# First embedding gate reordered by token tile, a new beginning without the spread row, and conv taps on TensorE in groups of ten

## What is computed

```python
h = rms_norm(x, pre_norm_g[0])                    # the beginning
z = h @ ret_w_in                                  # the heads: q, k, v, gate
a = einsum('bhid,bhjd->bhij', qb, kb) * dmask     # masked products of a head
...
x = x + rms_norm(y, post_norm_g[i])
x = x + (p[i] @ ple_w_proj[i]) * sigmoid(x @ ple_w_gate[i])   # the embedding gate
h = rms_norm(x, pre_norm_g[1]);  z = h @ mla_w_in             # what follows the first gate
...
ya = a_val * sigmoid(a_gate)
ya = causal_dwconv(ya, w_dw_a, b_dw_a)            # 31 taps, 512 channels = 4 tiles of 128
ya = silu(layer_norm(ya)) @ w_pw_a
ga, gb = sigmoid(gate_a), sigmoid(gate_b)         # gate strips: columns of the same w_in
```

## Time and profile before

| | |
|---|---|
| median of 3 runs | 875.16 us (875.09 to 876.24) |
| the profiled execution | 875.0 us, its span 873.2 us |
| granted clock of TensorE, mean | 0.996 |
| busy: PE, PEld, DVE, ACT, POOL | 858.1, 781.1, 662.8, 492.7, 50.3 us |
| first matmul of the span | at 1.33 us |
| read from HBM | 167.95 MB, 194 GB/s over the span |

### The profile page before, as it was taken

The page is one execution under the profiler, slowest core; times in us unless marked ns, Lnnn a source line. Parts: engine busy times, 40 slices in busy tenths (PEclk is TensorE's granted clock), DMA queues, the critical chain, the costliest instruction groups (busy, mean ns, idle before and its releaser), DMA issues.

```text
span 873.2 us, 15801 instructions
## 1 busy us (share of the span) xinstructions
PE 858.1 (98%) x5676; PEld 781.1 (89%) x5676; DVE 662.8 (76%) x928; ACT 492.7 (56%) x732; POOL 50.3 (6%) x61
## 2 busy tenths in 40 slices
PE   9999999999999999999999999999999999999995
PEld 7898999988868999999988889999998999999884
DVE  6869777686865786877866876899898788888566
ACT  5454545544646656656565446455753698888440
POOL 0018000000012000000000000070000000000000
PEclk9999999999999999999999999999999999999998
DMA  7857575669554656473738662634444465556541
GB/s 245 307 190 236 191 247 176 232 234 340 177 178 156 227 168 233 132 254 112 259 121 319 230 220 85 208 120 146 145 157 181 134 228 176 184 184 228 193 166 48
DMA packets 48433, 169.60 MB, mean 194 GB/s; under 512 B 5507, under 2 KB 6147, under 8 KB 48390
## 3 DMA queue, kind: packets, MB, share of 16 engines
q1 hardware_dynamic: 40612, 142.70, 48.2%
q10 hardware_dynamic: 7778, 26.32, 8.4%
HBM read 167.95 MB, written 1.05 MB: 194 GB/s over the span
## 4 chain that ended last, share of the span: by engine, by line
PE 87%; DVE 8%; ACT 2%; issue 2%; ACTq 0%; POOL 0%; DVEq 0%; POOLq 0%
PE bank L445 14%; PE bank L446 14%; PE bank L447 14%; PE bank L491 8%; PE bank L493 8%; PE bank L492 8%; PE bank L458 3%; PE bank L534 2%; PE bank L858 2%; DVE wlo L1441 1%; PE bank L766 1%; PE bank L654 1%; PE bank L655 1%; PE bank L656 1%; PE bank L769 1%
## 5 line engine op out<-in xcount | busy, mean ns | idle before, releaser
L934 ACT ACTIVATE whi<-raw 128x1024 fp32r<-128x1024 f32 (+1 forms) x251 | 259.6, 1040 | 223.7 <-PE bank L447 106.7
L1441 DVE TENSOR_TENSOR wlo<-raw,whi 128x1024 fp32r<-128x1024 f32 (+1 forms) x251 | 301.8, 1212 | 91.8 <-ACT whi L934 89.4
L445 PE MATMUL bank<-H,whi 128*128 128x256 f32 x904 | 261.6, 289 | 0.0
L447 PE MATMUL bank<-H,wlo 128*128 128x256 f32 x904 | 255.7, 283 | 0.0
L446 PE MATMUL bank<-H,whi 128*128 128x256 f32 x904 | 255.6, 283 | 0.0
L445 PEld LDWEIGHTS bank<-H,whi 128*128 128x128 f32 x904 | 173.2, 192 | 1.0 <-issue 0.4
L446 PEld LDWEIGHTS bank<-H,whi 128*128 128x128 f32 x904 | 173.3, 192 | 0.5
L447 PEld LDWEIGHTS bank<-H,wlo 128*128 128x128 f32 x904 | 173.1, 192 | 0.0
L491 PE MATMUL bank<-whi,Y 128*128 128x512 f32 x216 | 84.2, 390 | 0.0
L493 PE MATMUL bank<-whi,Y 128*128 128x512 f32 x216 | 84.1, 389 | 0.0
L492 PE MATMUL bank<-wlo,Y 128*128 128x512 f32 x216 | 84.1, 389 | 0.0
(11 more groups left out here) (259 smaller groups left out, 1310.6 us busy)
## 6 DMA issues: line engine op xcount, KB each, us to landing
ada_raw<-ada_in ACTq DMA_DIRECT2D x48, 512.0 KB, 5.2
raw<-w_head SPq DMA_DIRECT2D x47, 512.0 KB, 4.5
raw<-w_up SPq DMA_DIRECT2D x42, 512.0 KB, 3.4
...
```

The lines of the kernel that those rows point to most:

```text
L445: mm(o, whi[:, s, c], a[:, 0, :], start=start, stop=False)
L447: last = mm(o, wlo[:, s, c], a[:, 0, :], start=False, stop=stop)
L934: activation(whi[:, s, 0:n], block_in(b, n), ACT.Copy).then_inc(hi_done, 1)
L1441: tt(wlo[:, s, 0:n], block_in(b, n), f32(whi[:, s, 0:n]), ALU.subtract).then_inc(lo_done, 1)
```

## The change

1. The beginning. The spread row is gone (`row_spread`, L619). The gain of the first norm comes as 8 columns (`pre`, 128 x 8), and is applied after the transposes, when they are copied out of PSUM, as a scale per partition: four activations and four tensor_scalar per tile in place of one copy each. DVE scales X by the reciprocal alone. TensorE's `hold` runs 20 matmuls in a row. ACT and DVE split block 5 before the sine tables are waited for.
2. The heads. In each pass of the loop three blocks of the next head are split at its end in place of two, the two ada steps move back by one or two splits, and the mask of the head's product stands ahead of the split of block 11.
3. The first embedding gate. Tile 0 runs over both column halves (eight blocks), then tile 1. The split parts of blocks +4 to +7 (KEPT) lie in `Y`, which is free there, in place of the ring. The transposes of tile 0 for the next product stand between the second and third of tile 1's last four blocks. The order on ACT and DVE follows.
4. The convolution. Eight taps of channel tile 2 go from DVE to TensorE, which sums them in a second bank (`M3`); DVE adds that sum at the end. TensorE does its 39 taps in groups of 6, 10, 10, 10 and 3. The diagonals lie in `ada_raw`, in 16 slots.

The diff, cut to its core:

```diff
+DIAG_FIRST = [(0, 3), (1, 3), (2, 3), (3, 3), (4, 3), (3, 2)]
+DIAG_PASS = [(5 + k, 3) for k in range(8)] + [(7, 2), (11, 2)]
+DIAG_LAST = [(5, 2), (29, 3), (30, 3)]
+N_TAPS = 3 * CONV_K - 8
+N_DIAG = len(DIAG_FIRST) + 3 * len(DIAG_PASS) + len(DIAG_LAST)
+ON_PE = {(k, c) for k, c in DIAG_FIRST + DIAG_PASS + DIAG_LAST if c < 3}
...
+KEPT = [B_PG0 + 4 + j for j in range(4)]
...
-        DG = WK[:, 13:15, :].rearrange("p a t -> p (a t)").rearrange("p (r m) -> p r m", r=4)
+        DG = ada_raw[:].rearrange("p a n -> p (a n)").rearrange("p (r m) -> p r m", r=16)
...
+        def parts_of(b, n=1024):
+
+            if b in KEPT:
+                k = KEPT.index(b)
+                a = Y[:, 4 * k:4 * k + 4, :, :].rearrange("p k c t -> p (k c t)")
+                return a[:, 0:n], a[:, 1024:1024 + n]
+            return whi[:, b % RING, 0:n], wlo[:, b % RING, 0:n]
+
+        def used_first(b):
+
+            return b + 1 - RING * (b - RING in KEPT)
...
-            hold(PB[1], 4)
-            pe.wait_ge(row_a, 16)
-            for h in range(2):
-                last = mm(PB[0][:, 512 * h:512 * h + 512], ones[0:1, :], ROW_A[0:1, 512 * h:512 * h + 512], start=True,
-                          stop=True)
-            last.then_inc(row_spread, 1)
-            hold(PB[1], 3)
+            hold(PB[1], 20)
...
-            gate_rows(B_PG0, U_PLE0, 0)
-            gate_rows(B_PG0, U_PLE0, 1)
-            turn_tile(U_PRE1, 0, WT, PB[0])
+            token_pass(B_PG0, 0, 0, H, 0, 4, tile_waits(U_PLE0, 0))
+            token_pass(B_PG0, 0, 1, H, 0, 4)
+            token_pass(B_PG0, 1, 0, H, 0, 4, tile_waits(U_PLE0, 1))
+            for j in range(4):
+                if j == 2:
+                    turn_tile(U_PRE1, 0, WT, PB[0])
+                row_products(B_PG0 + 4 + j, half(2, 1, 1), 1, H, 2 * j, j == 0, j == 3).then_inc(pe_done, 1)
...
-            def tap(k, i=0, per=0):
-
-                if k == 0:
-                    pe.wait_ge(dve_free, V_WA + 4 + 2)
-                pe.wait_ge(tap_ready, k + 1 + per * i)
-                mm(M1[:, 0:T], DG[:, k % 4, :], CI[:, 3, bass.ds(k + per * i, T)], start=(per == 0 and k == 0),
-                   stop=(per == 0 and k == CONV_K - 1)).then_inc(conv_sum, 1)
+            def diagonals(taps, n0, i=0):
+
+                for n, (k, c) in enumerate(taps):
+                    pe.wait_ge(tap_ready, n0 + n + 1 + 10 * i)
+                    first, last = (k, c) in (DIAG_FIRST[0], DIAG_FIRST[5]), (k, c) in (DIAG_LAST[0], DIAG_LAST[2])
+                    x = CI[:, c, bass.ds(k + 8 * i, T)]
+                    mm(M1[:, 0:T] if c == 3 else M3[:, T:2 * T], DG[:, (n + (4 if n0 == 0 else 0)), :], x, start=first,
+                       stop=last).then_inc(conv_sum, 1)
...
                 strip(B_WP + j, halves(b)[j % 2], H)
-                for k in ((), (0, 1), (2, 3), (4,))[j]:
-                    tap(k)
+            pe.wait_ge(dve_free, V_WA + 4 + 2)
+            diagonals(DIAG_FIRST, 0)
             with pe.Fori(0, 3) as i:
                 for j in range(4):
                     if j % 2 == 0:
                         b = free_a(A_WG + j // 2, 2, i)
                     strip(B_WG + j, halves(b)[j % 2], H, 4, i)
-                    for k in (5 + 2 * j, 6 + 2 * j):
-                        tap(k, i, 8)
-            tap(29)
-            tap(30)
+                diagonals(DIAG_PASS, 6, i)
+            diagonals(DIAG_LAST, 36)
...
-                activation(WT[:, t, 0:512], b[:, 0:512], ACT.Copy).then_inc(plain_a, 1)
-
+                for k in range(4):
+                    activation(WT[:, t, P * k:P * k + P], b[:, P * k:P * k + P], ACT.Copy, scale=pre[:, k:k + 1])\
+                        .then_inc(plain_a, 1)
...
-            gate_evac(B_PJ0, B_PG0, U_PLE0, K_PG0, X_PLE0, True)
+            split(B_PJ0)
+            for q in range(2):
+                hi_quad(U_PLE0, 0, q, PB[2])
+            split(B_PJ0 + 1)
+            split(B_PG0)
+            for q in range(2):
+                hi_quad(U_PLE0, 1, q, PB[3])
+            for j in range(1, 5):
+                split(B_PG0 + j)
+            table(ACT.Sigmoid)
+            act.wait_ge(tok_done, K_PG0 + 1)
+            sigmoid(0, 0, 0, X_PLE0)
+            square_x(0, 0, X_PLE0 + 1)
+            act.wait_ge(tok_done, K_PG0 + 2)
+            sigmoid(1, 1, 0, X_PLE0)
+            square_x(0, 1, X_PLE0 + 2)
+            used(B_PG0 + 3)
+            sigmoid(2, 0, 1, X_PLE0)
+            split(B_PG0 + 5)
+            split(B_PG0 + 6)
+            square_x(1, 0, X_PLE0 + 3)
+            split(B_PG0 + 7)
             for q in range(2):
                 hi_quad(U_PRE1, 0, q, PB[0])
+            used(B_PG0 + 7)
+            sigmoid(3, 1, 1, X_PLE0)
...
-                pre_rows(t, PB[0][:])
+                ts(WT[:, t, :], X[:, t, :], rs[:, t, 0:1], None, ALU.mult).then_inc(wt_ready, 1)
+            dve.wait_ge(in_pre, 16)
             for t in range(2):
                 dve.wait_ge(turned_psum, 2 * t + 2)
-                nc.vector.tensor_copy(WT[:, t, 512:1024], PB[2 + t][:, 512:1024]).then_inc(plain_d, 1)
+                for k in range(4, 8):
+                    ts(WT[:, t, P * k:P * k + P], PB[2 + t][:, P * k:P * k + P], pre[:, k:k + 1], None, ALU.mult)\
...
-                for j in range(2, 12):
-                    split(B_HEAD + j, 1024, 12, i)
-                    if j == 2:
-                        used(B_HEAD + 1, 12, i)
-                        rope(GD[0], TA, TB, 0, Q, 1, dve_free, V_HEAD + 3, rope_ready, 2, (2, 2, 4), i)
-                    if j == 4:
-                        used(B_HEAD + 3, 12, i)
-                        rope(GD[1], TA, TB, 0, K, 2, dve_free, V_HEAD + 4, rope_ready, 4, (2, 2, 4), i)
-                    if j == 3:
-                        ada(0, 0, 0, 4, i)
-                    if j == 5:
-                        ada(1, 1, 0, 4, i)
+                used(B_HEAD + 1, 12, i)
+                rope(GD[0], TA, TB, 0, Q, 1, dve_free, V_HEAD + 3, rope_ready, 2, (2, 2, 4), i)
+                for j in range(3, 12):
                     if j == 8:
                         dve.wait_ge(at_ready, i + 1)
                         m = maskd[:, bass.ds(i, 1), :].rearrange("p a t -> p (a t)")
                         tt(AT[:, 0:T], M2[:, 0:T], m, ALU.mult).then_inc(atm_ready, 1)
                         tt(AT[:, T:T + P], M2[:, T:T + P], m[:, 0:P], ALU.mult).then_inc(atm_ready, 1)
+                    split(B_HEAD + j, 1024, 12, i)
+                    if j == 4:
+                        used(B_HEAD + 3, 12, i)
+                        rope(GD[1], TA, TB, 0, K, 2, dve_free, V_HEAD + 4, rope_ready, 4, (2, 2, 4), i)
+                    if j == 4:
+                        ada(0, 0, 0, 4, i)
+                    if j == 6:
+                        ada(1, 1, 0, 4, i)
+                    if j == 8:
                         ada(2, 0, 1, 4, i)
                     if j == 9:
                         ada(3, 1, 1, 4, i)
...
-            out_rows(B_RO, 16, 3, ROW_A, 32)
-            gate_start(B_PJ0, B_PG0, U_PLE0, X_PLE0, False)
+            out_rows(B_RO, 16, 3, ROW_A, 16)
+            lo_tile(U_PLE0, 0, PB[2])
+            split(B_PJ0)
+            split(B_PJ0 + 1)
+            split(B_PG0)
+            split(B_PG0 + 1)
+            split(B_PG0 + 2)
+            lo_tile(U_PLE0, 1, PB[3])
+            split(B_PG0 + 3)
+            update(0, 0, 0, X_PLE0)
+            split(B_PG0 + 4)
+            update(1, 1, 0, X_PLE0)
             dve.wait_ge(row_b, 16)
             root_of(1)
             pre_rows(0, ROW_B)
+            update(2, 0, 1, X_PLE0)
+            split(B_PG0 + 5)
             split(B_PG0 + 6)
             lo_tile(U_PRE1, 0, PB[0])
...
-            dve.wait_ge(conv_step, 3 * CONV_K)
+            dve.wait_ge(conv_step, N_TAPS)
+            dve.wait_ge(conv_sum, N_DIAG + 4)
+            tt(CO[:, 2, :], CO[:, 2, :], M3[:, T:2 * T], ALU.add).then_inc(conv_step, 1)
+            dve.wait_ge(conv_step, N_TAPS + 1)
```

127 lines of the change are left out of this document (73 added, 54 removed).

## The result

The changed kernel took 885.0 us (median of 4 executions, 882.8 to 886.8) against 875.6 for the kernel before (median of 4, 875.1 to 876.2): a ratio of 1.0105, with a 95% interval of 1.0092 to 1.0117. It is slower by 9.4 us, where 3.1 more were forecast (878.3 against 875.16), and the time lies above the range.

What follows compares the result with a forecast made beforehand. TensorE was taken to bound the kernel, busy 858.1 us of a span of 873.2. Sum: 875.0 - 2.5 (beginning) - 0.7 (mask) + 3.1 (gate) + 3.4 (taps) = 878.3 us, range 875.3 to 880.8.

Steps and rivals of the forecast that it cites:

- The sign: Whole kernel: the change was forecast to make it slower, with a chance of 0.70.
- The beginning (2.5 us): Start of the kernel: first product starts at about 10.1 in place of 12.37, a gain of 2.5 us.
- the third split: Head loop: carrying a third split ahead was said to have slack; no time was priced for it.
- The mask (0.7 us): Second head: mask ahead of a low-part split removes TensorE's 0.71 us wait, a gain of 0.7 us.
- The output rows (nothing priced): Stage behind the heads: the prediction gave no term for it, so 0 gained or lost.
- The gate (3.1 us): First embedding gate: 6.0 us of waits in place of 2.9, a loss of 3.1 us.
- The waits for blocks 6 and 7: Gate's first tile: 0.2 us late for block 5, 1.0 for block 6, 3.7 for block 7; 5.0 of waits.
- 1.0 was kept: Behind the gate: 1.0 us of waiting for blocks 2 and 3 of the next product, 0.84 in the kernel before.
- the old waits: First embedding gate of the kernel before: 2.9 us of TensorE waits, set against 6.0 in the changed one.
- The rival: Gate: idling for block 7 lowers TensorE's clock; half-speed work costs 1.0 to 2.0 us more, 879.9 in all; chance 0.30.
- The taps (3.4 us): Convolution: eight more taps on TensorE at 0.43 us each, grouping saves nothing, a loss of 3.4 us.

Runs made afterwards that it cites:

- mended: Changed kernel with block 7's low part ahead of the first update on VectorE in the first embedding gate: 879.3 us, ratio 1.0041.
- ada loads early: Changed kernel with the two ada loads after each retention head put back ahead of the third split on ScalarE: 880.0 us, ratio 1.0049.
- the version with the beginning and the mask: Kernel before with the new beginning and the mask ahead of block 11's low part, two splits carried over: 874.1 us, ratio 0.9983.
- that of 871.5 us: Changed kernel with ada loads ahead of the third split, the kernel before's gate, and 31 taps on TensorE: 871.5 us, ratio 0.9948.

## Why the prediction was wrong

The sign was right, and its own steps hold up except at two places.

- **The beginning (2.5 us): right in size, wrong in what it hangs on.** The first product starts at 10.17 (10.1 was said), the transposes at 7.96 (8.2). That the gain survives to the end of the first head is, by the traces, the work of the early split of block 5. The prediction said of the third split only that it had slack. 0.6 was gained beyond that, most of it the wait of 0.5 at 31.58 in the first head of the kernel before, which is gone.
- **The mask (0.7 us): right.** The second head gained 0.9, and no wait of TensorE is left in the heads.
- **The output rows (nothing priced): this is the step that failed.** The prediction put it so: "The other shifts in that loop (the third split ahead, the two ada steps) have slack, since TensorE waits nowhere else in the three looped heads." It looked for waits in the loop, and the damage is in the stage behind the loop. The split that was moved takes its whole place in ScalarE's queue with it; two loads stood behind it; and the rows that would have warned are those of the kernel before shown above: the first load lands at 183.8, and its step on VectorE starts at 184.12, with 0.3 us to spare. The edit cost 4.4 us in the changed kernel's profiled execution, 5.0 in the medians, and 3.7 when put into the kernel before. With this term the sum would have been 882.7, which by itself lies above the range.
- **The gate (3.1 us): mechanism right, one part sized too low, one not included.** The waits for blocks 6 and 7 are 4.9 us from matmul to matmul, where 5.0 were said (0.2, 1.0 and 3.7). Block 7's low part ended at 243.1, 14.6 behind the start of the pass, and the prediction had 14.5. Behind the gate 1.3 was left where 1.0 was kept. The rest is the clock, 2.3 us in this execution. With the 2.9 of the old waits off, these parts make 5.6 of the 5.9. The rival had named the cause and priced the resumed work at 1.0 to 2.0. It took the resumed work to be at half speed for up to 4 us, as at the start, and it was 4.9. With a chance of 0.30 it was thought less likely than no fall; the fall was seen in the changed kernel's profile and in those of three versions with the same gate, in none with a mended or an old one, where no wait in the gate was over 1.1 us. Whether it falls in every execution is open. Two of the changed kernel's four have a mean clock of 0.989 and 0.992, the other two 0.996 as the kernel before; but the profile with ada loads early also has 0.996, with 3.4 us at half speed in it. So a mean of 0.996 rules out a long fall and not a short one.
- **The taps (3.4 us): right.** 78 records as said, 12 in 2.76 us, and 3.5 us more up to the mean matmuls.

```profile
L881 PE MATMUL bank<-WK,ada_raw x78: 377/378/382, 571.9 to 623.1; 128*128 x60, 128*128 128x256 f32 x18
...
571.91 2.76 PE L881 MATMUL bank<-WK,ada_raw 128*128 128x256 f32 x12
```

The sum with the measured terms: 875.0 - 2.6 - 0.6 - 0.9 + 4.4 + 5.9 + 3.5 - 0.3 = 884.4, the profiled execution's own time. It has to come out so, since the terms are differences of starts on one engine. The medians are the test: taken out one at a time, the three losses gave 5.0 (ada loads), 6.5 (gate) and 3.9 (taps), 15.4 in all, and taken out together 13.5 (885.0 to 871.5). So they are separate terms to about 2 us.

What stays open is how much of the 2.7 us between the version with the beginning and the mask and that of 871.5 us is the third split in each head, and how much the new places of the ada steps and rotations on VectorE. They were not taken apart. Nor is it known why one execution's landing times differ from another's. The output rows lost between 2.6 and 5.2 us in the profiled executions of the changed kernel and of the five versions that have its order there, and the changed kernel's times spread over 4 us, where those of the 871.5 us version spread over 1.5.
